# A hybrid decoder trunk on one core: decode terms on ScalarE, the LRU scan behind an eviction, output weights loaded earlier, and the last down projection by token chunk

## What is computed

```python
x = x + 0.5 * SwiGLU_1(RMSNorm(x))
P = RMSNorm(x) @ w_in            # [lru_x | lru_y | ssd_z | ssd_xBC | ssd_dt]
lru = RMSNorm(rg_lru(conv4(lru_x)) * gelu(lru_y))
ssd = group_RMSNorm((ssd_scan(silu(conv4(xBC)), dt) + D * xs) * silu(z))
x = x + concat([lru, ssd]) @ w_out
x = x + 0.5 * SwiGLU_2(RMSNorm(x))
y = RMSNorm(x)
```

## Time and profile before

| | us |
|---|---|
| median of 3 runs | 2350.11 |
| lowest, highest | 2346.47, 2350.14 |
| profiled execution, its own time | 2347.34 |
| its span in the profile | 2345.6 |
| TensorE busy | 2263.4 (96%) |
| VectorE, ScalarE, GpSimd busy | 1036.1, 411.7, 796.9 |

### The profile page before, as it was taken

How to read it: one execution, slowest core, us unless ns; L and a number is a source line. 1 busy time by engine, 2 the same in 40 slices (tenths; PEclk the granted TensorE clock), 3 DMA queues, 4 the chain that set the end, 5 groups by cost and what they waited for, 6 DMA issues and landing times.

```text
span 2345.6 us, 31849 instructions
## 1 busy us (share of the span) xinstructions
PE 2263.4 (96%) x14361; PEld 2202.6 (94%) x14361; DVE 1036.1 (44%) x750; ACT 411.7 (18%) x415; POOL 796.9 (34%) x442
## 2 busy tenths in 40 slices
PE   7999999999999998899999989999999999999995
PEld 7999999999999898788788989999999999999995
DVE  6422123211334569867778565683231132212234
ACT  4100000000102221145454440121000001000011
POOL 4223332223323246534334543222223332223320
PEclk9999999999999999999999999999999999999998
DMA  4111111111113222211010422111111111111111
GB/s 146 46 46 46 46 46 53 46 46 46 46 40 105 99 73 108 92 41 48 30 41 30 162 82 75 49 43 53 46 46 46 46 46 54 46 46 46 43 42 78
DMA packets 46200, 138.87 MB, mean 59 GB/s; under 512 B 7528, under 2 KB 13160, under 8 KB 46064
## 3 DMA queue, kind: packets, MB, share of 16 engines
q1 hardware_dynamic: 44912, 135.78, 17.9%
q10 hardware_dynamic: 1152, 1.05, 0.2%
HBM read 118.19 MB, written 18.79 MB: 58 GB/s over the span
## 4 chain that ended last, share of the span: by engine, by line
PE 84%; DVE 9%; ACT 3%; DVEq 2%; issue 1%; DMA 0%; POOL 0%; POOLq 0%; SPq 0%; ACTq 0%
PE set L554 79%; DVE conv_out L1079 2%; DVE gate_a L1192 1%; DVE state L1091 1%; DVEq L1159 1%; PE set L726 1%; DVE state_add L1093 1%; PE pair L726 1%; DVEq L1194 1%; PE set L574 1%; PE pair L679 1%; DVE conv_in L978 0%; DVEq L1174 0%; DVE small L1095 0%; PE pair L709 0%
## 5 line engine op out<-in xcount | busy, mean ns | idle before, releaser
L443 POOL TENSOR_SCALAR w_hi<-w_raw 128x1024 fp32r<-128x1024 f32 (+1 forms) x188 | 218.6, 1163 | 1354.5 <-PE set L554 1302.1
L445 POOL TENSOR_TENSOR w_lo<-w_raw,w_hi 128x1024 fp32r<-128x1024 f32 (+1 forms) x188 | 456.7, 2429 | 28.6 <-issue 1.3
L554 PE MATMUL set<-x_hi,w_hi 128*128 128x344 f32 x2112 | 450.2, 322 | 12.2 <-DVE x_lo L982 12.2
L554 PE MATMUL set<-x_lo,w_hi 128*128 128x344 f32 x2112 | 448.8, 321 | 0.0
L554 PE MATMUL set<-x_hi,w_lo 128*128 128x344 f32 x2112 | 446.8, 320 | 0.0
L554 PEld LDWEIGHTS set<-x_hi,w_hi 128*128 128x128 f32 x2112 | 356.8, 189 | 12.9 <-issue 10.2
L554 PEld LDWEIGHTS set<-x_lo,w_hi 128*128 128x128 f32 x2112 | 358.2, 189 | 0.0
L554 PEld LDWEIGHTS set<-x_hi,w_lo 128*128 128x128 f32 x2112 | 352.8, 188 | 0.0
L978 DVE TENSOR_TENSOR up<-set,rstd 128x1032 f32<-128x1032 f32 x43 | 53.0, 1233 | 419.7 <-PE set L554 419.7
L554 PE MATMUL set<-u_hi,w_hi 128*128 128x344 f32 x864 | 200.8, 341 | 26.8 <-DVE lru_in L978 9.4
L554 PE MATMUL set<-h_lo,w_hi 128*128 128x344 f32 x1056 | 224.2, 320 | 0.0
(11 more groups left out here) (223 smaller groups left out, 2407.2 us busy)
## 6 DMA issues: line engine op xcount, KB each, us to landing
w_raw<-in_gate_up SPq DMA_DIRECT2D x88, 512.0 KB, 3.5
w_raw<-in_w_in SPq DMA_DIRECT2D x36, 512.0 KB, 3.6
w_raw<-in_down SPq DMA_DIRECT2D x32, 512.0 KB, 3.5
w_raw<-in_w_out SPq DMA_DIRECT2D x16, 512.0 KB, 3.7
w_raw<-in_down SPq DMA_DIRECT2D x16, 384.0 KB, 3.2
x<-in_xt SPq DMA_DIRECT2D x8, 516.0 KB, 8.2
x_kept<-x SPq DMA_DIRECT2D x8, 516.0 KB, 4.8
mixed<-power SPq DMA_DIRECT2D x8, 516.0 KB, 2.7
```

Of the source, the lines that this page charges most:

```text
L443: pool.tensor_scalar(w_hi[s][:, 0:n], w_raw[s][:, 0:n], 1.0, 0.0, ALU.mult, ALU.add)
L445: pool.tensor_tensor(w_lo[s][:, 0:n], w_raw[s][:, 0:n], w_hi[s][:, 0:n].bitcast(F32), ALU.subtract).then_inc(split, 1)
L554: end = pe.matmul(out[:, c, 0:CH], w[s][:, k * P:(k + 1) * P], x[:, kx, c * CH:(c + 1) * CH], start=(first and n == 0), stop=(last and n = ...
```

## The change

Four edits. (1) The decode terms move from two GpSimd instructions of 128x1024 to 16 ScalarE instructions of 128x128, each with its own scale per partition; the small product `small` goes to VectorE (`decode_scale`), and `decode(q-7)` stands behind `convolve(q)`. (2) `lru_scan` is cut in two: the input products stay, the scan itself stands behind `lx`'s eviction, the second `mask` and the first `skip_and_state`. (3) SP loads three `w_out` tiles before the first residual copy and keeps three ahead; four of the eight `ssd_lo` tiles and the first `ssd` reciprocal move behind the first output tiles. (4) In the last block the down units m = 2 to 7 are split into buffers of their own (`split_resident`, `down_hi`, `down_lo`) and multiplied chunk by chunk, 18 pieces of 18 matmuls; squares, sums, root, scaling and stores of a chunk run beside the next chunk's pieces. y is scaled in place in `x`.

```diff
+            for m in range(3):
+                load(("ol", m))
             for m in range(KT):
-                load(("ol", m))
                 sp.wait_ge(s_split, m + 1)
                 if m >= 4:
                     sp.wait_ge(squared["ssd1"], m - 3)
                 sp.dma_start(f2.x[:, m, :], d.x_kept[:, m, :]).then_inc(x3_landed[m], 16)
+                if m + 3 < KT:
+                    load(("ol", m + 3))
...
-                    for m in range(KT):
+                    for m in range(WHOLE if tag == "2" and b == LAST else KT):
                         split_unit(("d" + tag, b, m))
 
+            def split_resident(m):
+
+                u, _, nk = plan.units["d2", LAST, m]
+                n = nk * P
+                pool.wait_ge(landed[u % 2], 16 * (u // 2 + 1))
+                pool.tensor_scalar(dw_hi[m][:], w_raw[u % 2][:, 0:n], 1.0, 0.0, ALU.mult, ALU.add)
+                pool.drain()
+                pool.tensor_tensor(dw_lo[m][:], w_raw[u % 2][:, 0:n], dw_hi[m][:].bitcast(F32),
+                                   ALU.subtract).then_inc(split, 1)
+
...
-                if q >= 7:
-                    decode_terms(q - 7)
             split_unit(("z", 0))
-            decode_terms(5)
             split_unit(("z", 1))
-            decode_terms(6)
             split_unit(("lx", 0))
-            decode_terms(7)
...
             ffn("2")
+            pool.wait_ge(used, U(("u2", NH - 1)) + 1)
+            for m in range(WHOLE, KT):
+                split_resident(m)
...
+            def last_sum(c):
+                pe.wait_ge(added["final"], (KT - 1) * (c + 1))
+                if c == 2:
+                    pe.wait_ge(root_taken, 1)
+                pe.matmul(pair[:, c % 2, 0:CH], ones[:], f2.tot[:, c * CH:(c + 1) * CH],
+                          start=True, stop=True).then_inc(summed["final"], 1)
+
+            for n in range(2):
+                pe.wait_ge(set_free[n], plan.taken[n])
+            for c in range(CHUNKS):
+                here = slice(c * CH, (c + 1) * CH)
+                for m in range(WHOLE, KT):
+                    if c == 0:
+                        pe.wait_ge(split, U(("d2", LAST, m)) + 1)
+                    else:
+                        pe.wait_ge(piece_read, (c - 1) * (KT - WHOLE) + m - WHOLE + 1)
+                    bank = sets[(m - WHOLE) // 3][:, (m - WHOLE) % 3, 0:CH]
+                    for k in range(n_last):
+                        for n, (w, x) in enumerate(((dw_hi, f2.hh), (dw_hi, f2.hl), (dw_lo, f2.hh))):
+                            end = pe.matmul(bank, w[m][:, k * P:(k + 1) * P], x[:, k, here],
+                                            start=(k == 0 and n == 0), stop=(k == n_last - 1 and n == 2))
+                    end.then_inc(piece_done, 1)
+                    if c and m == WHOLE + 1:
+                        last_sum(c - 1)
+            last_sum(CHUNKS - 1)
 
...
+            def decode_terms(t):
+
+                g, s = t // (KT // GROUPS), t % 4
+                xd = xbc[:, 4 + t, PROMPT:T]
+                act.wait_ge(state_landed[s], 16 * (t // 4 + 1))
+                if t == 0:
+                    act.wait_ge(bc_landed, 64)
+                if t >= 2:
+                    act.wait_ge(dec_y, t - 1)
+                for b in range(DEC):
+                    act.activation(state[s][:, b, :], state[s][:, b, :], ACT.Copy, scale=dec_a[:, t, b:b + 1])
+                dve_small = small[:, t % 2, :]
+                act.wait_ge(small_ready, t + 1)
+                for b in range(DEC):
+                    last = act.activation(upd[t % 2][:, b, :], b_dec[g][:, b, :], ACT.Copy, scale=dve_small[:, b:b + 1])
+                last.then_inc(dec_terms, 1)
...
+                if q >= 7:
+                    decode_terms(q - 7)
                 act.wait_ge(convolved, q + 1)
...
             for t in range(EARLY):
+                if t == 0:
+                    decode_terms(5)
+                    decode_terms(6)
                 freed(("z", t))
                 act.activation(z_early[t][:], z_early[t][:], ACT.Silu).then_inc(z_silu, 1)
+                if t == 0:
+                    decode_terms(7)
 
             def lru_gates(t):
...
+            def piece_square(c, m):
+                here = slice(c * CH, (c + 1) * CH)
+                if m < WHOLE:
+                    if c == 0:
+                        freed(("d2", LAST, m))
+                else:
+                    act.wait_ge(piece_read, c * (KT - WHOLE) + m - WHOLE + 1)
+                if m >= 3:
+                    act.wait_ge(added["final"], (KT - 1) * c + m - 2)
+                elif c and m:
+                    act.wait_ge(added["final"], (KT - 1) * c)
+                to = f2.c[m % 2] if m else f2.tot
+                act.activation(to[:, here], f2.x[:, m, here], ACT.Square).then_inc(squared["final"], 1)
+
+            def piece_root(c):
+                act.wait_ge(summed["final"], c + 1)
+                act.activation(rstd[:, c * CH:(c + 1) * CH], pair[:, c % 2, 0:CH], ACT.Sqrt, bias=eps[:, 0:1],
+                               scale=1.0 / DM).then_inc(root_taken, 1)
+
+            for c in range(CHUNKS):
+                for m in range(KT):
+                    piece_square(c, m)
+                    if c and m == 4:
+                        piece_root(c - 1)
+            piece_root(CHUNKS - 1)
 
         def vector(dve):
...
-                    decode(q - 7)
+                if q >= 7:
+                    decode_scale(q - 7)
                 convolve(q, raw2[q % 2], acc2[q % 2])
                 if q == 3:
                     dt_finish()
-            decode(4)
+                if q >= 7:
+                    decode(q - 7)
+            decode_scale(5)
+            decode_scale(6)
             scaled(("z", 0), z_early[0][:], rstd)
             decode(5)
+            decode_scale(7)
             decode(6)
             scaled(("z", 1), z_early[1][:], rstd)
...
+            def lru_scan(t):
                 dve.drain()
                 dve.tensor_tensor(gate_a[:, PROMPT:T], gate_a[:, PROMPT:T], gate_x[:, PROMPT:T], ALU.add)
...
                 mask(c, 0)
                 if c:
-                    lru_scan(c - 1)
+                    lru_scan_input(c - 1)
                     dve.wait_ge(tails, XT + c)
                 scaled(("lx", c), lraw[:], rstd)
                 mask(c, 1)
                 skip_and_state(c, 0)
+                if c:
+                    lru_scan(c - 1)
...
                     reciprocal("lru", tl)
+            def ssd_low(k):
+                low(s_lo[:, k, :], s_hi[:, k, :], xbc[:, 4 + k, :], V_SSD + k, s_hi_done, k + 1, s_split)
+
             dve.drain()
-            for k in range(KT):
-                low(s_lo[:, k, :], s_hi[:, k, :], xbc[:, 4 + k, :], V_SSD + k, s_hi_done, k + 1, s_split)
+            for k in range(4):
+                ssd_low(k)
             for m in range(KT):
                 dve.drain()
                 scaled(("ol", m), rstd[:], tl)
                 dve.wait_ge(x3_landed[m], 16)
                 dve.drain()
                 dve.tensor_tensor(f2.x[:, m, :], f2.x[:, m, :], rstd[:], ALU.add)
-                if m == 0:
+                if m < 2:
+                    ssd_low(4 + 2 * m)
+                    ssd_low(5 + 2 * m)
+                if m == 2:
...
+
+            def piece_add(c, m):
+                here = slice(c * CH, (c + 1) * CH)
+                if m >= WHOLE:
+                    n = c * (KT - WHOLE) + m - WHOLE
+                    dve.wait_ge(piece_done, n + 1)
+                    tile = f2.x[:, m, here]
+                    dve.scalar_tensor_tensor(tile, sets[(m - WHOLE) // 3][:, (m - WHOLE) % 3, 0:CH], 0.5, tile,
+                                             ALU.mult, ALU.add).then_inc(piece_read, 1)
+                dve.wait_ge(squared["final"], c * KT + m + 1)
+                if m:
+                    dve.drain()
+                    dve.tensor_tensor(f2.tot[:, here], f2.tot[:, here], f2.c[m % 2][:, here],
+                                      ALU.add).then_inc(added["final"], 1)
+
+            def piece_scale(c, k):
+                here = slice(c * CH, (c + 1) * CH)
+                if k == 0:
+                    dve.wait_ge(root_taken, c + 1)
+                    dve.reciprocal(rstd[:, here], rstd[:, here])
+                    dve.drain()
+                dve.scalar_tensor_tensor(f2.x[:, k, here], f2.x[:, k, here], vecs[:, V_FINAL + k:V_FINAL + k + 1],
+                                         rstd[:, here], ALU.mult, ALU.mult).then_inc(y_done_final, 1)
+
+            for c in range(CHUNKS):
                 for m in range(KT):
-                    residual(f2, b, m)
-                    if b == LAST:
-                        dve.drain()
-                        add("final", m, f2)
-            reciprocal("final", rstd)
+                    piece_add(c, m)
+                    if c and m >= 4:
+                        piece_scale(c - 1, 2 * (m - 4))
+                        piece_scale(c - 1, 2 * (m - 4) + 1)
```

(19 more changed lines are left out.)

46 lines of the change are left out of this document (22 added, 24 removed).

## The result

| | us |
|---|---|
| kernel before, median of 4 runs | 2350.12 (2346.47 to 2350.77) |
| changed kernel, median of 4 runs | 2333.53 (2332.72 to 2335.35) |
| ratio, 95% interval | 0.9937 [0.9923, 0.9952] |
| profiled execution, its own time and span | 2335.35, 2333.6 |
| TensorE busy; VectorE, ScalarE, GpSimd busy | 2271.4 (97%); 1016.3, 451.7, 741.4 |

The change makes the kernel 0.6% faster. To see what each edit gave I cut both traces at the same three products of TensorE and took differences of their start times: P0, the first product after the wait for `dt_rows` (813.52 before, 812.23 after); P1, the second `seg` product of slot 0 (977.64, 962.90); P2, the first product after the wait for `total_s`, a unit of the output projection (1371.41, 1379.23); P3, the sum of FFN 2's norm (1573.14, 1571.83).

A forecast was written before the change was run, and what follows sets the result against it. TensorE's chain of matmuls was taken as the bound, with gains only at its idle gaps, low clock and tail. -15.7 + 19.1 - 8.9 - 10.7 = -16.2 on 2347.3 gave 2331 us, range 2304 to 2344.

The forecast's parts named there:

- B: The SSD/LRU slots: with the scan behind the eviction, lru_in and e waits go but gate waits; +19.1 us.
- A: xBC tiles and first slot: decode terms on ScalarE end the conv_in waits, early_z 1 comes late; -15.7 us.
- The term of waits: Slots, within the +19.1: four longer by +8.0 together, the first two by +0.7 each, the last by +2.9 us.
- The term of clock: Slots, within the +19.1: the wait of 4.9 at gate costs clock in four slots, 4 x 1.7 = +6.8 us.
- C: Output projection: weights loaded ahead remove the waits of 6.21 and 1.05 and the clock loss behind the first; -8.9 us.
- D: The end: last block by chunk leaves 14.5 instead of 28.8 behind the last piece, with 3.6 new costs; -10.7 us.
- That the clock holds at `gate`: Rival for the slots: the waits at gate come but cost no clock; 2324 us, chance 0.20.
- That VectorE is in time: Rival for the slots: VectorE reaches gate in time or nearly; 2312 us, at its bound 2297, chance 0.20.
- That the hand-over doesn't gain: Rival for the xBC tiles: ScalarE's 16 instructions cost 5.9 or more, z eviction late; 2339 us, chance 0.11.
- The slower case: Rival for the slots: the clock, once down at gate, stays down; 2354 us at 15 us each, chance 0.05.

The follow-up runs named there:

- short_total: The changed kernel with GpSimd's LRU sum of squares inside the slots cut from 1032 columns to 8; 2310.23 us.
- quiet: The changed kernel with the scan at its old place and GpSimd's seg_terms and LRU sum of squares moved behind the split of ly; 2292.24 us.
- filler: The changed kernel with products that nobody reads put on TensorE into the wait at the gate products; 2318.58 us.
- terms_alone: The kernel before with only the decode terms moved to ScalarE (edit 1); 2331.28 us, ratio 0.9934.

## Why the prediction was right, step by step

**The sum.** 2331.0 was forecast, 2333.5 measured. Each term has its sign and nearly its size; against the profiled execution of before the forecast was -16.2, and the four stretches give -10.7, with -1.3 more ahead of P0, where nothing was changed. B is the larger part of the difference, A the rest. That the medians of the first series (-16.6) come so near the forecast's -16.2 is luck. 3.0 us of clock were lost in A's stretch at places that no edit touches (below); without them the four stretches give -13.7, close to what the later medians of before give.

**A, -15.7 forecast, -13.4 measured.** The hand-over did what the step said: no wait for `conv_in`, and one of 4.63 for `early_z` 1 where 4.7 was worked out. The 16 instructions take 4.69 a tile, against 4.4 in the sum. One takes 0.388 and not 0.37, and they start 0.294 apart and not 0.27. The Trainium skill's figures (ScalarE: Activation LUTs, What ACT_TABLE_LOAD costs) gave an estimated 4.7, and the trace agrees with that rather than with mine. It cost TensorE no wait beside the xBC tiles, since there a tile takes 11.45 on ScalarE and VectorE (ScalarE's second group of eight starts at 917.04 and 928.49) and 11.37 on TensorE. The rest of the difference is clock, lost ahead of the first decode term (879.5): behind the same wait of 2.55 for `dt_rows` TensorE needs 22.84 to its next wait in the changed kernel, 21.31 before; and from 847 to 854 its granted clock is 0.76, where it was 1.00 before, which cost another 1.5. In short_total and quiet neither happened, and the stretch is 147.7, that is -16.4.

**B, +19.1 forecast, +22.6 measured.** The mechanism is right in every part: the gap at `gate` (4.9 forecast, 4.69), 2 in slots 1 and 2 (1.93), and 2.81 in slot 7. Its two prices were both off. The term of waits, 8.0 + 1.4 + 2.9 = 12.3, measured 8.9: a slot of 3 to 6 without clock loss would be 41.39 + 2.76 = 44.15 long, 1.4 more than before and not 2.0, since TensorE's own work in a slot is 39.5 and not the 39.8 that I had left after taking the waits away, and the wait was 0.2 shorter; slots 1 and 2 grew by 0.3 and not 0.7, slot 7 by 2.8. The term of clock, 4 x 1.7 = 6.8, measured 13.7. It was mis-sized twice: after a wait of 4.69 a slot lost 2.8, 3.2, 1.7 and 2.7 (46.93, 47.39, 45.82, 46.84, less the 41.39 of slot 2 and the 2.76 by which the wait is longer), not 1.7, and the waits of 1.93 and 2.81, which the step had free because the gaps under 2.8 in region A showed no loss, lost 1.7 once in slots 1 and 2 and 1.7 in slot 7 (79.13 from its gate product to P2, and 77.48 in filler). The two errors, -3.4 and +6.9, have opposite signs: that B came within 3.5 is in part luck. A row of the kernel before that shows no loss after a gap was no proof that such gaps are free.

**C, -8.9 forecast, -9.1 measured**, in the whole change and alone.

**D, -10.7 forecast, -10.7 measured**, in both. 14.5 was forecast behind the last piece and 14.65 came, though its parts were off both ways: the step has 3.6 for the last store, where rows 1 give 3.8 (2341.8 to 2345.6), and from the last scaling's end (2330.79) to the end of the span it was 2.8; the sum (1.53 and not 1.2) and the eight scalings (3.99 and not 3.7) took longer. Of its new costs `h_lo` was 0.75 late (1.0) and the first piece 1.37 (1.4).

**The rivals.** That the clock holds at `gate` is refuted: it fell in all four slots. That VectorE is in time is refuted by 25.4 us of waits. That the hand-over doesn't gain is refuted by terms_alone. The slower case needed 11 us at the low level after each wait to win nothing, and 15 for its 2354; the losses of 1.7 to 3.2 are 3.4 to 6.4 us at half the clock. Edit 2 by itself does make the kernel slower, by 0.95%, and the other three carry it.
